# A recurrence's chunk inverse as products of 32x32 blocks, and four steps of its loop in another order

## The reference

```python
def step(S, inp):
    r_t, d_t, k_t, v_t, kk_t, b_t = inp
    sa = jnp.einsum('bhij,bhj->bhi', S, -kk_t)
    S = S * d_t[:, :, None, :] + sa[..., None] * b_t[:, :, None, :] + v_t[..., None] * k_t[:, :, None, :]
    return S, jnp.einsum('bhij,bhj->bhi', S, r_t)
...
for d in range(N_DIR):
    wd = -jax.nn.softplus(-(w0[d] + jnp.tanh(w_in[d]) @ w2[d])) - 0.5
    ad = jax.nn.sigmoid(a0[d] + a_in[d] @ a2[d])
    kd = k * (1.0 + (ad - 1.0) * k_a)
    ...
    bonus = bonus + jnp.sum(r4 * kd4 * r_k4, axis=-1, keepdims=True) * v4
```

## Time and profile before

| what | us |
|---|---|
| three runs: median (lowest to highest) | 3640.97 (3639.27 to 3643.91) |
| the profiled execution, its own time | 3642.95 |
| its span in the trace | 3641.1 |
| the recurrence: six pairs, from the first pair's `zw` to the last pair's last step | 372.5 to 725 |

### The profile page before, as it was taken

One profiled execution on the slowest core, in us unless ns is written; L12 is line 12 of the kernel. 1 busy time (PEld: TensorE's weight loads), 2 busy tenths in 40 slices (PEclk: granted clock), 3 DMA queues, 4 the chain that ended last, 5 costly groups with the idle time before them and its releaser, 6 DMA issues.

```text
span 3641.1 us, 76911 instructions
## 1 busy us (share of the span) xinstructions
PE 3527.3 (97%) x28942; PEld 3286.5 (90%) x28942; DVE 2395.7 (66%) x3378; ACT 1633.3 (45%) x2222; POOL 349.5 (10%) x401
## 2 busy tenths in 40 slices
PE   8999999999999999889999999999999799999997
PEld 8998899889999999889888888889999788888886
DVE  6977667665665467966666665676666665656566
ACT  6456333344444434654444444443444443434344
POOL 5000233200020000211000000010000300000003
PEclk9999999999999999999999999999999899999998
DMA  6544222145555555445565556555554465655564
GB/s 249 160 153 145 77 72 83 61 139 184 198 184 185 185 174 167 146 145 179 184 192 184 190 184 194 183 188 185 173 162 152 129 194 185 191 184 190 185 193 153
DMA packets 165417, 606.14 MB, mean 166 GB/s; under 512 B 18384, under 2 KB 18512, under 8 KB 164992
## 3 DMA queue, kind: packets, MB, share of 16 engines
q1 hardware_dynamic: 164016, 598.25, 50.9%
q10 hardware_dynamic: 1040, 3.16, 0.2%
q0 software_dynamic: 192, 2.23, 0.2%
HBM read 601.47 MB, written 2.10 MB: 166 GB/s over the span
## 4 chain that ended last, share of the span: by engine, by line
PE 85%; DVE 9%; ACT 3%; issue 2%; POOL 1%; DMA 0%; DVEq 0%; ACTq 0%; POOLq 0%
PE bank L332 25%; PE bank L317 14%; PE bank L318 14%; PE bank L319 13%; PE bank L335 13%; PE bank L1276 5%; DVE w_lo L306 3%; ACT w_hi L297 1%; POOL x_norm_acc L426 0%; DVE xa L1854 0%; ACT X L2667 0%; PE bank L1482 0%; DVE nrm_kk L992 0%; ACT x L1153 0%; DVE xa L1847 0%
## 5 line engine op out<-in xcount | busy, mean ns | idle before, releaser
L297 ACT ACTIVATE w_hi<-raw 128x1024 fp32r<-128x1024 f32 x1130 | 1162.3, 1053 | 889.0 <-PE bank L319 517.7
L306 DVE TENSOR_TENSOR w_lo<-raw,w_hi 128x1024 fp32r<-128x1024 f32 x1130 | 1367.5, 1249 | 108.2 <-ACT w_hi L297 108.0
L332 PE MATMUL bank<-hid,w_hi 128*128 128x512 f32 x2048 | 644.2, 396 | 1.4 <-DVE hid L2097 1.2
L317 PE MATMUL bank<-hx,w_hi 128*128 128x256 f32 x1568 | 459.7, 293 | 12.0 <-DVE w_lo L306 12.0
L335 PEld LDWEIGHTS bank<-hid,w_lo 128*128 128x128 f32 x2048 | 384.7, 188 | 90.9
L318 PE MATMUL bank<-hx,w_hi 128*128 128x256 f32 x1568 | 445.3, 284 | 0.0
L319 PE MATMUL bank<-hx,w_lo 128*128 128x256 f32 x1568 | 445.0, 284 | 0.0
L335 PE MATMUL bank<-hid,w_lo 128*128 128x256 f32 x2048 | 402.4, 278 | 0.0
L317 PE MATMUL bank<-u,w_hi 128*128 128x256 f32 (+1 forms) x1280 | 366.6, 286 | 9.8 <-DVE w_lo L306 9.8
L318 PE MATMUL bank<-u,w_hi 128*128 128x256 f32 (+1 forms) x1280 | 368.3, 288 | 0.0
L319 PE MATMUL bank<-u,w_lo 128*128 128x256 f32 (+1 forms) x1280 | 367.3, 287 | 0.0
(11 more groups left out here) (455 smaller groups left out, 6260.6 us busy)
## 6 DMA issues: line engine op xcount, KB each, us to landing
raw<-stream SPq DMA_DIRECT2D x1130, 512.0 KB, 4.0
x_raw<-xT SPq DMA_DIRECT2D x4, 512.0 KB, 7.3
mem_raw<-memT ACTq DMA_DIRECT2D x4, 512.0 KB, 10.4
x_res<-xT POOLq DMA_DIRECT2D x1, 2048.0 KB, 8.3
out<-X SPq DMA_DIRECT2D x4, 512.0 KB, 2.6
cst<-consts SPq DMA_DIRECT2D x1, 1504.0 KB, 13.4
w_sb<-w ACTq DMA_DIRECT2D x1, 384.0 KB, 5.2
a_sb<-a ACTq DMA_DIRECT2D x1, 384.0 KB, 5.5
```

Of the source, the lines that this page charges most:

```text
L297: nc.scalar.activation(w_hi[:, slot], raw[:, slot], ACT.Copy).then_inc(hi_ready, 1)
L306: nc.vector.tensor_tensor(w_lo[:, slot], raw[:, slot], w_hi[:, slot].bitcast(F), ALU.subtract).then_inc(lo_ready, 1)
L317: nc.tensor.matmul(dst, w_hi[:, slot, j], hi, start=first, stop=False)
L332: nc.tensor.matmul(bank[:], w_hi[:, slot, i], moving[:, kt].rearrange("p a t -> p (a t)"), start=kt == 0, stop=False)
```

## The change

Levels 1 to 4 only ever join blocks inside a 32x32 block on the diagonal. The change holds `mt`, `tm`, `x` and `u` for them as 32 columns per chunk (`sub_part`, tiles `mts`, `tms`, `xss`, `uss`: 128 partitions by 128) and multiplies 32x32 by 32x32 (`quarters`): four blocks stand on the 128 partitions (two heads by two halves), so that a product is 16 matmuls and not 8. All that reads or writes these tiles on ScalarE, VectorE and GpSimd has 128 elements per partition and not 256.

M is needed twice in the first group of products: `sub_gram` forms its diagonal 32x32 blocks (64 rows deep, 32x32 out, 16 matmuls), and for `mt` the full 64x64 product is made besides, from which VectorE masks the off-diagonal blocks for level 5 (`last`, a new VectorE step; GpSimd no longer makes that mask). Level 5 runs in 64x64 blocks with 32 moving columns (`last_level`): X and U. ScalarE puts the whole `u` together out of the 32-column one (`whole`, two ACTIVATEs a direction) before VectorE adds the last U; GpSimd clears half of `x` (`xz`).

Four orders change. On TensorE, direction 1's U product of a level is issued after direction 0's X product of the next level. On VectorE, the three sums `ks`, `ksr`, `q` move from ahead of the first group's masks to behind the second group's. On VectorE the `split_lo` at the head of a pair moves behind the step `end`, and on ScalarE the `split_hi` at the head moves behind `vtok0`. Ahead of a pair's first tanh ScalarE runs a tanh on one column (`tanh_warm`).

```diff
@@ pool_rwkv
-                ident = four(const("istack"))
+                ident = four_sub(const("sub_eye"))
...
+                    rw_o.done(nc.gpsimd.memset(w["x"][:, :, inner(1 - d)], 0.0), f"xz{d}")
                 for l in LV:
-                    if l > 1:
+                    if 1 < l < LEVELS - 1:
@@ act_rwkv
             with act.Fori(0, PAIRS) as p:
-                split_hi(act, pair_tile(p, 0).later(), (0,))
+                nc.scalar.activation(tanh_warm[:], tanh_warm[:], ACT.Tanh).then_inc(warmed, 1)
...
                 rw_a.done(nc.scalar.activation(v_tok[:], value_part(bank_of(0, 2), 0), ACT.Copy), "vtok0")
+                split_hi(act, pair_tile(p, 0).later(), (0,))
...
-                        rw_a.done(nc.scalar.activation(w["x"][:], value_part(bank_of(d, 1), 0), ACT.Copy), f"X{l}_{d}")
+                        x = w["xs"][:] if l < LEVELS - 1 else w["x"][:, :, inner(d)]
+                        rw_a.done(nc.scalar.activation(x, sub_part(bank_of(d, 1)), ACT.Copy), f"X{l}_{d}")
+                        if l == LEVELS - 1:
+
+                            need(act, rw_v, f"U{l - 1}_{d}", p)
+                            for b in range(2):
+                                block = cst[:, CCOL["sub_block"] + b:CCOL["sub_block"] + b + 1]
+                                last = nc.scalar.activation(w["u"][:, :, inner(b)], w["us"][:], ACT.Identity, scale=block)
+                            rw_a.done(last, f"whole{d}")
@@ dve_rwkv
             with v.Fori(0, PAIRS) as p:
-                split_lo(v, pair_tile(p, 0).later(), (0,))
...
+                split_lo(v, pair_tile(p, 0).later(), (0,))
+                dve_pair_gate(v, p, 0)
+                split_lo(v, pair_tile(p, 0).later(), (1,))
...
+                    rw_v.done(nc.vector.scalar_tensor_tensor(w["ml"][LEVELS - 1][:], value_part(bank_of(d, 0), 0), -1.0, four(last_mask),
+                                                             ALU.mult, ALU.mult), f"last{d}")
+                    rw_v.done(nc.vector.scalar_tensor_tensor(w["mt"][:], sub_part(bank_of(d, 0), T), -1.0, four_sub(sub_mask), ALU.mult, ALU.mult), f"mt{d}")
...
@@ pe_rwkv
+                def quarters(bank, lhs, rhs):
+
+                    for c in range(NCH):
+                        for q in range(P // SUB):
+                            r = slice(SUB * q, SUB * q + SUB)
+                            last = nc.tensor.matmul(bank[r, SUB * c:SUB * c + SUB], lhs[r, c], rhs[r, c], start=True, stop=True)
+                    return last
+
+                def sub_gram(bank, o, lhs, rhs):
+
+                    for c in range(NCH):
+                        for q in range(P // SUB):
+                            h, b = halves()[q // 2], slice(SUB * (q % 2), SUB * (q % 2) + SUB)
+                            last = nc.tensor.matmul(bank[SUB * q:SUB * q + SUB, o + SUB * c:o + SUB * c + SUB], lhs[h, c, b], rhs[h, c, b], start=True, stop=True)
+                    return last
+
+                def last_level(bank, lhs, rhs):
+
+                    for c in range(NCH):
+                        last = heads2(bank[:, SUB * c:SUB * c + SUB], lhs[:, c], rhs[:, c])
+                    return last
...
-                    rw_p.done(each(bank_of(d, 0), w["bbd"], w["abd"]), f"mt{d}")
+                    each(bank_of(d, 0), w["bbd"], w["abd"])
+                    rw_p.done(sub_gram(bank_of(d, 0), T, w["bbd"], w["abd"]), f"mt{d}")
...
-                    rw_p.done(each(bank_of(d, 2), w["abd"], w["bbd"]), f"m{d}")
+                    rw_p.done(sub_gram(bank_of(d, 2), 0, w["abd"], w["bbd"]), f"m{d}")
...
                 for l in LV:
...
+                    level_x(l, 0)
+                    if l > 1:
+                        level_u(l - 1, 1)
+                    level_x(l, 1)
+                    level_known(l, 0)
+                    if l < LEVELS - 1:
+                        level_t(l, 0)
+                    level_u(l, 0)
+                    level_known(l, 1)
+                    if l < LEVELS - 1:
+                        level_t(l, 1)
+                    else:
+                        level_u(l, 1)
```

More of the change, by code:

```diff
@@ L34 @@
 CH = 64
+SUB = 32
 NCH = T // CH
@@ L154, in constants @@
     up, lo = s[:, None] < c, s[:, None] > c
+    sub, cs = i % SUB, np.arange(SUB)[None, :]
+    sub_up, sub_lo = sub[:, None] < cs, sub[:, None] > cs
+    sub_levels = [(sub[:, None] >> (l + 1) == cs >> (l + 1)) & (sub[:, None] >> l != cs >> l) for l in range(LEVELS - 1)]
     levels = [(s[:, None] >> (l + 1) == c >> (l + 1)) & (s[:, None] >> l != c >> l) for l in range(LEVELS)]
@@ L934, in build @@
             w = {}
-            for k, n in enumerate(("abd", "rbd", "bbd", "kbd", "mt", "tm", "brt", "btok", "ktok", "nkatv", "kat", "krt", "u", "x")):
-                w[n] = at(f"{n}{d}", o + K * k, [P, NCH, CH])
-            w["ml"] = {l: at(f"ml{l}_{d}", o + 13 * K + K * l, [P, NCH, CH]) for l in range(1, LEVELS)}
+            for k, n in enumerate(("abd", "rbd", "bbd", "kbd", "", "", "brt", "btok", "ktok", "nkatv", "kat", "krt", "u", "x")):
+                if n:
+                    w[n] = at(f"{n}{d}", o + K * k, [P, NCH, CH])
+            w["ml"] = {l: at(f"ml{l}_{d}", o + 13 * K + K * l, [P, NCH, SUB if l < LEVELS - 1 else CH]) for l in range(1, LEVELS)}
+            for n, b in (("mt", 4 * K), ("us", 4 * K + 512), ("tm", 5 * K), ("xs", 5 * K + 512)):
+                w[n] = at(f"{n}s{d}", o + b, [P, NCH, SUB])
             for k, n in enumerate(("e1", "e2", "e3", "th")):
@@ L1016, in build @@
                      + [f"{n}{d}" for d in D2 for n in ("e1", "e2", "e3")] + [f"btok{d}" for d in D2] + [f"ktok{d}" for d in D2]
-                     + [f"X{l}_{d}" for l in LV for d in D2] + [f"SA{s}_{d}" for s in ST for d in D2])
+                     + [f"X{l}_{d}" for l in LV if l < LEVELS - 1 for d in D2]
+                     + [f"{n}{d}" for d in D2 for n in (f"X{LEVELS - 1}_", "whole")] + [f"SA{s}_{d}" for s in ST for d in D2])
         rw_p = Steps(sem("rwkv_pe"), [f"{n}{d}" for d in D2 for n in ("zw", "za")] + ["vtok0"]
@@ L1072, in value_part, with four_sub, sub_part, inner @@
             return bank[:, T * k:T * k + T].rearrange("p (c i) -> p c i", c=NCH)
+        def four_sub(ap):
+            return ap.unsqueeze(1).broadcast_to([P, NCH, SUB])
         def level(l):
-            return four(const("levels")[:, CH * l:CH * l + CH])
+            return four_sub(const("sub_levels")[:, SUB * l:SUB * l + SUB])
+        def sub_part(bank, o=0):
+            return bank[:, o:o + NCH * SUB].rearrange("p (c i) -> p c i", c=NCH)
+        def inner(d):
+            return slice(SUB * d, SUB * d + SUB)
         def halves():
@@ L1229, in dve_rwkv @@
                             need(v, rw_p, f"T{l}_{d}", p)
-                            rw_v.done(nc.vector.tensor_tensor(w["tm"][:], w["tm"][:], value_part(bank_of(d, 0), 0), ALU.add), f"T{l}_{d}")
-                        need(v, rw_p, f"U{l}_{d}", p)
[L1232 to L1236, removed]
+                            rw_v.done(nc.vector.tensor_tensor(w["tm"][:], w["tm"][:], sub_part(bank_of(d, 0)), ALU.add), f"T{l}_{d}")
+                        if d == 1 and l == TILE_2[0] - 1:
+                            dve_pair_gate(v, p, 2)
+                        if d == 1 and l in TILE_2:
+                            split_lo(v, pair_tile(p, 2).later(), (TILE_2.index(l),))
+                        need(v, rw_p, f"U{l}_{d}", p)
+                        if l == LEVELS - 1:
+                            need(v, rw_a, f"whole{d}", p)
+                        u = w["us"][:] if l < LEVELS - 1 else w["u"][:, :, inner(1 - d)]
+                        rw_v.done(nc.vector.tensor_tensor(u, u, sub_part(bank_of(d, 2)), ALU.add), f"U{l}_{d}")
                 for s in ST:
@@ L1327, in pe_rwkv, with level_x @@
                 go(GO_GRAM)
-                for l in LV:
[L1329 to L1349, removed]
+                def level_x(l, d):
+                    w = dirs[d]
+                    if l < LEVELS - 1:
+                        need(pe, rw_o, f"ml{l}_{d}", p)
+                    if l == 1:
+                        need(pe, rw_o, f"t1_{d}", p)
+                        need(pe, rw_a, f"ktok{d}", p)
+                    else:
+                        need(pe, rw_v, f"T{l - 1}_{d}", p)
+                    rw_p.done((quarters if l < LEVELS - 1 else last_level)(bank_of(d, 1), w["ml"][l], w["tm"]), f"X{l}_{d}")
@@ new lines, in level_known, with level_t @@
+                def level_known(l, d):
+                    need(pe, rw_a, f"X{l}_{d}", p)
+                    if l == 1:
+                        need(pe, rw_o, f"u1_{d}", p)
+                        need(pe, rw_a, f"btok{d}", p)
+                        need(pe, rw_v, f"krtv{d}", p)
+                    else:
+                        need(pe, rw_v, f"U{l - 1}_{d}", p)
+                def level_t(l, d):
+                    w = dirs[d]
+                    rw_p.done(quarters(bank_of(d, 0), w["us"], w["xs"]), f"T{l}_{d}")
```

64 lines of the change are left out of this document (40 added, 24 removed).

## The result

| what | before | after |
|---|---|---|
| median of four runs each, us | 3641.34 | 3718.45 (3715.90 to 3721.68) |
| ratio, with its 95% interval | | 1.0211 (1.0198 to 1.0224) |
| the profiled execution, its own time, us | 3642.95 | 3720.84 |
| its span; mean granted clock of TensorE | 3641.1; 0.988 | 3719.0; 0.966 |
| first `zw` to the last pair's first `SA`, us | 340.24 | 415.98 |

The account below looks back on a forecast made before the run. TensorE, busy 97% of the span, was taken as the bound; −3.75 (levels) + 1.2 (first group) − 0.6 (head) = −3.15 us a pair, six times −18.9, and −0.9 give −19.8: 3621 us, 8-in-10 range 3609 to 3648.

Parts of the forecast that it names:

- The 32x32 product: Levels 1 to 4: a product of 32x32 blocks takes 0.27 us, between bounds of 0.23 and 0.93.
- a cycle of 1.72: Levels: one direction's chain of X product, ScalarE's copy, T product and VectorE's sum takes 1.72 us a level.
- The argument from the sequencer and from two tiles side by side: Level products: matmuls issue at most 16 to 23 ns each and two tiles start within 10 ns, supporting 0.27 us.
- The sum over the levels: Levels 1 to 5 of a pair: 11.5 us where 15.3 stood, −3.75 us a pair.
- The slower rival: Products of levels 1 to 4: one start every 29 ns over the whole array, 0.93 us each; total 3725, chance 0.10.
- The clock rival: Levels: TensorE, idle by turns, runs at half clock; total about 3638, chance 0.07.
- The first group: First group of products: four of 0.466 us, four of 0.27, plus 1.05 for tile shape changes; +1.2 us a pair.
- The head: Head of a pair: VectorE's chain starts 1.1 us earlier; −0.6 us a pair, −1.5 in the first.
- What was put at no cost: GpSimd's half tiles, VectorE's first masks, the moved sums `ks`, `ksr`, `q`, and `split_hi` behind `vtok0`: no added time.
- Splits on VectorE: Levels 2 and 3: a VectorE split of 1.22 us beside four sums adds 0.6 us to each level.

Follow-up runs that it names:

- bf16_and_half: The changed kernel with level operands in bf16 and half of the matmuls of levels 1 to 4 left out: 3625.53 us beside 3640.40.
- the bf16 levels: The changed kernel with the operands of the levels (ml, x, us, xs, tms) held in bf16: 3651.72 us.
- the head-only kernel: The kernel before with only the moves at a pair's head (both splits, one-column tanh) and of the three sums: 3635.48 us, ratio 0.9986.
- the filling run: The changed kernel with five of seven filling units behind the third group moved into the levels: 3728.33 us, ratio to before 1.0237.
- sixteen columns: The kernel before with level operands in bf16 and each level product cut into 16 moving columns on 64x64 tiles: 3727.30 us.
- half of the blocks: The changed kernel with each product of levels 1 to 4 issuing only 8 of its 16 matmuls: 3658.08 us.

## Why the prediction was wrong, step by step

**The 32x32 product: right.** 0.27 us forecast. In the timeline of the changed kernel:

```profile
619.95 0.75 PE L1340 MATMUL bank<-tms,ml 32*32 32x32 f32 x64
620.81 0.45 PE L1340 MATMUL bank<-xss,uss 32*32 32x32 f32 x32
621.09 0.75 PE L1340 MATMUL bank<-uss,xss 32*32 32x32 f32 x32
...
622.04 0.19 PE L1340 MATMUL bank<-tms,ml 32*32 32x32 f32 x1
```

The T product (620.81) is followed by the U product 0.28 us later. Direction 0's X product of level 1 starts at 619.95 and that of level 2 at 622.04: 2.09 us, where the forecast has a cycle of 1.72. In this pair the end of a piece falls into the U product, whose weight loads break off for 0.17 us at 621.35, 126 records ahead of the first long stop. In four of the other pairs the cycle is 1.82 or 1.83 us, 0.1 over the forecast. The argument from the sequencer and from two tiles side by side held. The 32 records start 9 ns apart on average, so the floor of 25 ns between matmul starts that the Trainium skill gives ("TensorE: Matmul & The Clock Gate", section "Wait — 56ns, not 53.3ns?") does not hold across the tiles of the array; the measurement decides.

**The sum over the levels: the step that failed.** "Four levels are 6.9 us ... In all 11.5 for 15.3." This multiplied a rate that holds for the first 2 to 3 us by six products and four levels, and never asked where the instructions come from. 416 matmuls in the levels are 6.5 pieces, at 4 us each 26 us of supply; measured 24.1 to 25.6 (the first piece is there already). The forecast term was −3.75 us a pair, the measured one +9.3 to +10.8. I had read the earlier trace rows as the sequencer's speed; it is its speed on instructions that it already holds.

**The slower rival: nearly its number, not its mechanism.** "One start every 29 ns over the whole array" gave 3725. Starts are 9 ns apart, and the extra time is in stops. The nearness is chance: a 64x64 matmul takes 58 ns, and a piece of 64 in 4.0 us is 62 ns a matmul, so that both count doubled matmuls at about the old price.

**The clock rival: right, and on top.** I gave it 0.07 and argued that "no single wait here passes 1 us". In the change the stops do pass it; run bf16_and_half shows that none has to. The granted clock in the levels is 0.57 to 0.64, under the 0.95 that the prediction named as a sign of being wrong. In the change the low clock costs 2.0 to 4.0 us a pair in the steps, 14.4 in all, and it is what keeps the bf16 levels, 1 to 4 us shorter than those of before, from gaining anything.

**The first group: right.** +1.2 forecast; +1.04 in three of the six pairs (6.69 us from its start to the second group, for 5.65); the others have 0.9, 1.2 and 1.7 more than the same pair before. The timeline:

```profile
601.75 0.68 PE L1322 MATMUL bank<-abd,bbd 64*64 64x64 f32 x16
602.37 0.46 PE L1348 MATMUL bank<-abd,bbd 64*32 64x32 f32 x32
602.75 0.68 PE L1322 MATMUL bank<-abd,kbd 64*64 64x64 f32 x16
```

A 64x64 product and one of `sub_gram` take 1.00 us together. With 0.466 for the one and 0.27 for the other, 0.26 are left for two changes, 0.13 each (forecast 0.15); no run has the product of `sub_gram` at 0.27 by itself, but its 32 records start 8.5 ns apart on average. So 64 rows by 64 and 64 rows by 32 do behave as two modes, and the rule of the Trainium skill ("TensorEngine Tiling (Array Packing)", section "Key Properties") that a change of mode drains TensorE agrees with the trace.

**The head: right.** −0.6 forecast, −0.61 measured in every pair but the first; `th` is read by VectorE at 592.58, 1.33 us after `zw` where it was 2.34, 1.0 us earlier for a forecast of 1.1. First pair: −1.5 forecast, −1.78 measured: TensorE's wait for `e_end` falls from 4.15 us to

```profile
385.46 0.68 PE L1322 MATMUL bank<-abd,bbd 64*64 64x64 f32 x16 [2.37 <-DVE e_end L1230]
```

**What was put at no cost** was at no cost: the head-only kernel has the same 5.65 us for each group as before.

**Splits on VectorE.** I priced them at 0.6 us in two levels. In bf16_and_half, where no stop is in the way, the waits behind them are 1.09 and 0.87 us, there at the low clock. Right in kind, too small.

**What stays open.** Whether a steady 32x32 kernel would keep its clock if the levels were filled densely: the filling run was itself short of instructions and cannot say. And why a piece takes 4 us when its transfer takes 1.0: in the three kernels with the most stops the transfer starts 1.5 to 1.6 us on average after TensorE last went on, lasts about 1.1, and TensorE goes on 1.2 to 1.6 us after its end; what passes in the first and the last part no trace shows.

## What to carry to other kernels

Count instructions as a resource: in this kernel TensorE gets 256 of them (64 f32 matmuls, 128 bf16 ones) about every 4 us, so that splitting matmuls smaller pays only as long as 64 of them take longer than that, however fast each becomes. Look at the time marked as waiting for nothing, and count the records between two such gaps: a constant count that ignores the program's structure is a supply, not a wait. And shortening the dense part of a loop into one that idles by turns can halve the clock of what comes behind it, as it did here; price that with the dense parts behind at half speed before counting the gain.

## What the hardware showed that I had not expected

- The instructions arrive in pieces of 16,384 bytes on a queue of their own; a piece takes about 1 us of transfer, and when TensorE has used it up it goes on 4.0 us on average after it last went on (3.5 to 4.9 over all pairs; 4.0 and 4.1 on average with filling and with sixteen columns, 4.3 and 4.5 in the few cases with bf16 and with half of the blocks). There are such stops with f32 and bf16, and with 32x32 and 64x64 tiles.
- The kernel before stood just below that limit: 4.15 us of level time per 64 matmuls. Taking its 0.39 us waits away brought a stop of 0.8 to 1.2 us in three of six pairs.
- 32 records of 32x32 start within 0.28 us, 9 ns apart.
- The granted clock fell after 3.2 us in which TensorE was busy two thirds of the time and never waited more than 0.34 us at once.
